# Masking the attention scores: a fill by the vector engine ahead of the row maxima, in place of two products on TensorE

## The chip, the cores and the metric

The kernel runs on one core of a Trainium2 chip. A core has engines that run side by side, each through its own list of instructions in order: TensorE (PE in the profile; PEld is its loading of weights) multiplies matrices, VectorE (DVE) and ScalarE (ACT) work on elements, GpSimd (POOL) does small jobs, and SyncE (SP) starts transfers. They wait for each other by counting semaphores. Products land in PSUM, a memory of eight banks that DVE and ACT read and write too; everything else lies in SBUF.

The metric is the device time of one execution in microseconds (us): before the change 1562.58 us, the median of three runs (1562.52 to 1562.68).

## The reference

Two transformer blocks over 512 tokens of width 1024. The change touches only the attention of the first block. There 16 meta tokens stand in front of the 512, and each of 8 heads has two maps of queries and keys (64 wide) and a value of 128. A token sees the meta tokens and all chunks of 64 tokens up to its own:

```python
cid = jnp.where(pos < N_META, 0, (pos - N_META) // CHUNK + 1)
...
s = jnp.einsum('bqhmd,bkhmd->bhmqk', qb, kf)
mask = cid[None, :] <= qc[:, None]
p = jax.nn.softmax(jnp.where(mask, s, NEG_INF), axis=-1)
a = p[:, :, 0] - lam * p[:, :, 1]
return jnp.einsum('bhqk,bkhe->bqhe', a, vf)
```

Queries are taken 128 at a time, which is two chunks. Against the keys up to the end of their own 128 tokens, the first 64 queries may not see the last 64 keys; the rest of that rectangle is allowed. So per tile of 128 queries and per map the mask is one square: query rows 0 to 63 by the last 64 key columns.

## The kernel before

The program is one fixed list of instructions for each engine, written by hand. Stages follow one another: a convolution's inputs (the GLU), then ten turns that make q, k, v and a gate for each head and do the attention of the head before, then the projections of block one, its feed-forward part, and block two. Weights come in pieces of 512 KB; ACT copies each into a high part (`wh`, line 1405), DVE subtracts to get a low part (`wl`, line 1956), and PE multiplies three times (high by high, high by low, low by high; line 677).

Turn h (lines 927 to 963 on PE) makes the four parts of head h, `part(h, 0)` to `part(h, 3)` (q, k, v, gate), 48 products each, and between them does the attention of head a = h - 1, in four tiles t of 128 queries. A part goes to one PSUM tile (`psP[0]`) that ACT must have emptied (`empty`, line 1483) before the next part begins. The steps of head a:

- `scores(a, t)` on PE (line 837): q by k for both maps, into `psS`. Then, for each map, the product of two constants `mki` and `mkk` (line 858) adds -1e30 to the masked square. At t = 0 the meta tokens' own scores follow (line 861).
- `maxima(a, t)` on DVE (line 2089): the row maxima of both maps in one reduction (line 2093; line 2095 for t = 3; line 2098 for the meta rows).
- `exps(a, t)` on ACT (line 1501): exponentials and their sums, which need the maxima.
- `combine(a, t)` on DVE (line 2101): the difference of the two maps. PE transposes it (`probs`, line 879), ACT copies it, PE multiplies by the values (`outputs`, line 894).
- the norm of head a - 1's output runs through the same turn: `variances` (DVE, 2119), a square root on ACT (`norm_outputs`, 1547), `roots` (DVE, 2126), a scaling on ACT (1553).

What fixes the order around the change: in each turn DVE does maxima 0 and 1, the gate of an earlier head, combine 0 and 1, the low part of a weight piece, four taps of the depthwise convolution (line 2059, 31 taps in each of eight groups, spread over the turns by fixed counts), variances, two taps, maxima 2, roots, combine 2, five taps, maxima 3, three taps, combine 3, a second low part, seven taps. ACT does exps 0 and 1, the high part of a piece, the copy and squares of a head's output, `empty(h, 0)`, the values, exps 2, a copy, the square root (with a load of its function table), the scaling, `empty(h, 1)`, a copy, exps 3, another high part, `empty(h, 2)`, a copy, `empty(h, 3)`. So `part(h, 2)` on PE, which needs `empty(h, 1)`, stands behind maxima 2 by way of ACT. `own` is a helper that makes an engine wait until its own last instruction has finished.

Of the kernel before, what the change touches and what calls it, by code (L numbers as in the profile page):

```python
# [20 lines left out]
T = S + NM  # L21
HT = T // 2
# [11 lines left out]
BIG = 1.0e30  # L34
# [67 lines left out]
def program(nc, A, out):  # L102
    f32, f32r = mybir.dt.float32, mybir.dt.float32r
# [5 lines left out]
    def evacuated(gi):  # L109

        return EV[gi], CREDIT + EV[:gi + 1].count(EV[gi])
# [8 lines left out]
    with ExitStack() as ctx:  # L120
# [25 lines left out]
        scores_ps = ctx.enter_context(nc.psum_tensor("psS", [128, 4, 512], f32))  # L146
# [5 lines left out]
        def at(name, shape, dt=f32, start=None):  # L152
            if start is not None:
                place[0] = start
            n = 4
            for d in shape[1:]:
                n *= d
            t = nc.alloc_sbuf_tensor_at(name, shape, dt, offset=place[0])
            place[0] += -(-n // 32) * 32
            assert place[0] <= nc.sbuf_usable_end, (name, place[0] - nc.sbuf_usable_end)  # L160
            return t
# [27 lines left out]
        PW = [NM + 128 * (t + 1) for t in range(TT)]  # L189
# [32 lines left out]
        pmeta = at("pmeta", [NM, 2, NM])  # L222
        stat = at("stat", [128, 32])
        var = at("var", [128, 2, TT + 1])
        mki = at("mki", [128, 128], f32r)
        mkk = at("mkk", [128, 64], f32r)

# [236 lines left out]
        def span(t, g, c0, n):  # L466

            if isinstance(g, int):
                return t[:, g, c0:c0 + 2 * n].rearrange("p (a b) -> p a b", a=2)
            return t[:, ds(g, 1), c0:c0 + 2 * n].rearrange("p o (a b) -> p (o a) b", a=2)  # L470
# [178 lines left out]
        def _(pe):  # L649
            mm, tr = nc.tensor.matmul, nc.tensor.transpose  # L650
# [134 lines left out]
            for k in range(KT):  # L785
                tr(scores_ps[:, 3, 128 + NM * k:128 + NM * (k + 1)], mn[:, 128 * k:128 * (k + 1)], ident[0:NM, 0:NM])
                ins = tr(scores_ps[:, 3, 256 + NM * k:256 + NM * (k + 1)], mrow[:, 128 * k:128 * (k + 1)], ident[0:NM, 0:NM])
# [10 lines left out]
            for k in range(KT):  # L798
# [3 lines left out]
                for half in range(2):  # L802
                    for p, (W, Y) in enumerate(((wh, xh), (wh, xl), (wl, xh))):
                        for a in range(2):
                            ins = mm(psP[half][:, a, 0:HT], W[:, 0, half, k, :], Y[:, k, a * HT:(a + 1) * HT],  # L805
                                     start=(k == 0 and p == 0), stop=(k == KT - 1 and p == 2))
# [15 lines left out]
            for b in range(2):  # L822
                for v in range(4):
                    o = (4 * b + v) * 2 * FG
                    ins = tr(psP[0][:, 1, o:o + 2 * FG], frow[:, b, v, :], ident[0:2 * FG, 0:2 * FG])
# [11 lines left out]
            def scores(a, t):  # L837
                if a:
                    pe.wait_ge(s_ex, 4 * a + (0, 0, 1, 3)[t])
                elif t >= 2:  # L840
                    pe.wait_ge(s_ex, t - 1 if t == 2 else 3)
                if t == 0:
                    pe.wait_ge(s_ea, evacuated(2 * (N_HEAD + 2 * a) + 1)[1])
                maps = [slice(64 * m, 64 * m + 64) for m in range(2)]
                last = []
                for m, P in enumerate(maps):
                    q = qkv[P, a % 2, 0, NM + 128 * t:NM + 128 * (t + 1)]
                    K = qkv[P, a % 2, 1, :]
                    if t < 3:
                        bank = scores_ps[:, 2 * (t % 2) + m, :]  # L850
                        mm(bank[:, 0:PW[t]], q, K[:, 0:PW[t]], start=True, stop=False)
                        last.append(bank[:, PW[t] - 64:PW[t]])
                    else:
                        mm(scores_ps[:, 2 * m, 0:HT], q, K[:, 0:HT], start=True, stop=True)
                        mm(scores_ps[:, 2 * m + 1, 0:HT], q, K[:, HT:T], start=True, stop=False)
                        last.append(scores_ps[:, 2 * m + 1, HT - 64:HT])
                for m, P in enumerate(maps):
                    ins = mm(last[m], mki[P, :], mkk[P, :], start=False, stop=True)
                if t == 0:
                    for m, P in enumerate(maps):  # L860
                        ins = mm(scores_ps[0:NM, m, PW[0]:PW[0] + NM], qkv[P, a % 2, 0, 0:NM], qkv[P, a % 2, 1, 0:NM], start=True,
                                 stop=True)
                ins.then_inc(s_qk, 1)
# [63 lines left out]
            for h in range(NH + 2):  # L927
                a, b, c = h - 1, h - 2, h - 3
                if b >= 0:
                    probs(b, 3)  # L930
                if 0 <= a < NH:
                    scores(a, 0)
                    scores(a, 1)
# [12 lines left out]
                if 0 <= a < NH:  # L946
                    if h < NH:
                        values(a)
                    scores(a, 2)
                    probs(a, 0)  # L950
# [998 lines left out]
        def _(dve):  # L1949
            V = nc.vector  # L1950
            own = Own(dve, s_v)
# [83 lines left out]
            for z in (vm, pm, vr):  # L2035
                V.memset(z[:], 0.0)
            V.memset(var[:], 1.0)
            V.memset(mki[:].bitcast(f32), 0.0)
            own(V.memset(mkk[:].bitcast(f32), 0.0))
            for m in range(2):  # L2040
                V.memset(mki[64 * m:64 * m + 1, 0:64].bitcast(f32), 1.0)
                V.memset(mkk[64 * m:64 * m + 1, :].bitcast(f32), -BIG)


            tap = [0]
# [43 lines left out]
            def maxima(a, t):  # L2089
                dve.wait_ge(s_qk, 4 * a + t + 1)  # L2090
                if t < 3:
                    b = 2 * (t % 2)
                    ins = V.tensor_reduce(stat[:, 2 * t:2 * t + 2], scores_ps[:, b:b + 2, 0:PW[t]], AX, ALU.max, negate=True)  # L2093
                else:
                    ins = V.tensor_reduce(stat[:, 6:8], scores_ps[:, :, 0:HT].rearrange("p (m a) b -> p m a b", m=2),
                                          mybir.AxisListType.XY, ALU.max, negate=True)
                if t == 0:
                    ins = V.tensor_reduce(stat[0:NM, 16:18], scores_ps[0:NM, 0:2, PW[0]:PW[0] + NM], AX, ALU.max, negate=True)
                ins.then_inc(s_ma, 1)
# [39 lines left out]
            for h in range(NH + 2):  # L2139
                n, a, b, c = N_HEAD + 2 * h, h - 1, h - 2, h - 3  # L2140
                if 0 <= a < NH:
                    maxima(a, 0)
                    maxima(a, 1)
# [15 lines left out]
                if 0 <= a < NH:  # L2159
                    maxima(a, 2)  # L2160
# [34 lines left out]
            for n in range(N_CO, N_CO + 4):  # L2195
                lo(n + 1)
                for half in range(2):
# [3 lines left out]
                    t = nf[:, g % 2, 0:T3]  # L2201
                    if g >= 2:
                        dve.wait_ge(s_ml, g - 1)
                    ins = V.scalar_tensor_tensor(t.rearrange("p (a b) -> p a b", a=2), span(sgc, g, 0, H3), 1.0,
                                                 ALLP[gi % 4][:, :, 0:H3], ALU.add, ALU.mult)
# [418 lines left out]
            for k in range(1, KT):  # L2624
                ins = V.tensor_tensor(sacc[:, 0, 0:S], sacc[:, 0, 0:S] if k > 1 else ysq[:, 0, :], ysq[:, k, :], ALU.add)
# [60 lines left out]
```

## Time and profile before

| | us |
|---|---|
| median of three runs | 1562.58 |
| span of the profiled execution | 1562.9 |
| PE busy | 1532.4 |
| DVE busy | 1126.0 |
| ACT busy | 665.2 |

The profile gives the profiled execution's time as the span from its first to its last instruction, 1562.9 us, 0.3 us above the median of the runs; nothing outside the span is listed. A row of the time order is: start, length, engine, line, operation, output and inputs, shapes, how many are merged, and in brackets the idle time before it with what ended it. A window's row is: from and to, length, busy time and count of PE, PEld, DVE, ACT and POOL, the granted clock of PE (1.00 is full), the transfers' share and GB/s. Lengths of single products are modelled, so PE's cost is better read from one start to the next.

### The profile page before, as it was taken

To read this page: it belongs to the slowest core of one execution; us is meant where nothing else is said; L and a number is where in the kernel's file an instruction comes from. 1 tells how busy PE (TensorE), PEld (TensorE's weight loads), DVE (VectorE), ACT (ScalarE), POOL (GpSimd) and SP (SyncE) were. 2 spreads that over 40 slices of the span, in tenths; PEclk is the share of its full clock that TensorE was granted. 3 is DMA by queue.
4 is the path that set the end of the run, shared out by engine and by line. 5 is a ranking of instruction groups with operands and counts; after the bars stand their busy time and mean duration, and the time that the engine had idled before them with its cause. 6 is when DMAs were issued, how large, how long until landed. Compare 5 with 4: busy or idle time off the path is not lost.

```text
span 1562.9 us, 25443 instructions
## 1 busy us (share of the span) xinstructions
PE 1532.4 (98%) x9972; PEld 1368.4 (88%) x9972; DVE 1126.0 (72%) x1590; ACT 665.2 (43%) x1035; POOL 35.3 (2%) x66
## 2 busy tenths in 40 slices
PE   7999999999999999999999999999999999999998
PEld 7998988898999999999988888878788888888887
DVE  5899888888655577777774548897748988787123
ACT  5223455556662443334333344753646432333112
POOL 0000000100000000000000001000000000000000
PEclk9999999999999999999999999999999999999999
DMA  6323222222223333232223243322122233232321
GB/s 176 82 81 91 72 55 55 55 73 64 68 68 103 87 86 103 81 106 82 77 70 108 77 121 87 81 54 68 55 82 81 81 107 106 82 107 94 108 81 54
DMA packets 235295, 131.63 MB, mean 84 GB/s; under 512 B 20921, under 2 KB 228677, under 8 KB 235221
## 3 DMA queue, kind: packets, MB, share of 16 engines
q1 hardware_dynamic: 234836, 130.40, 29.7%
q8 instruction: 52, 0.85, 0.2%
q0 software_dynamic: 384, 0.20, 0.1%
q14 instruction: 23, 0.18, 0.0%
HBM read 128.48 MB, written 2.10 MB: 84 GB/s over the span
## 4 chain that ended last, share of the span: by engine, by line
PE 77%; DVE 15%; ACT 6%; issue 1%; DMA 0%; DVEq 0%; ACTq 0%
PE psP L677 25%; PE psS L677 22%; PE psP L742 8%; DVE conv L2059 7%; PE psS L1353 4%; PE psP L1353 4%; PE psP L699 4%; PE psP L1044 3%; DVE wl L1956 2%; PE psP L1221 1%; ACT prob L1512 1%; PE psS L1221 1%; ACT wh L1405 1%; PE psP L805 1%; DVE stat L2093 1%
## 5 line engine op out<-in xcount | busy, mean ns | idle before, releaser
L1956 DVE TENSOR_TENSOR wl<-raw,wh 128x2048 fp32r<-128x2048 f32 x124 | 284.1, 2291 | 178.3 <-ACT wh L1405 176.5
L677 PE MATMUL psP<-xh,wh 128*128 128x258 f32 (+2 forms) x1296 | 320.3, 312 | 13.8 <-ACT qkv L1499 8.9
L1405 ACT ACTIVATE wh<-raw 128x2048 fp32r<-128x2048 f32 x124 | 237.2, 1913 | 209.5 <-PE psS L1353 74.3
L677 PE MATMUL psP<-xh,wl 128*128 128x258 f32 (+2 forms) x1296 | 315.9, 308 | 0.0
L677 PE MATMUL psP<-xl,wh 128*128 128x258 f32 (+2 forms) x1296 | 315.3, 308 | 0.0
L677 PEld LDWEIGHTS psP<-xh,wh 128*128 128x128 f32 x1296 | 211.8, 191 | 30.3 <-issue 8.0
L677 PEld LDWEIGHTS psP<-xl,wh 128*128 128x128 f32 x1296 | 211.3, 190 | 12.0 <-issue 0.2
L677 PEld LDWEIGHTS psP<-xh,wl 128*128 128x128 f32 x1296 | 211.2, 190 | 11.9
L677 PE MATMUL psS<-xh,wh 128*128 128x258 f32 (+2 forms) x768 | 186.7, 307 | 0.4 <-DVE hT L1985 0.4
L677 PE MATMUL psS<-xh,wl 128*128 128x258 f32 (+2 forms) x768 | 185.9, 307 | 0.0
L677 PE MATMUL psS<-xl,wh 128*128 128x258 f32 (+2 forms) x768 | 185.6, 306 | 0.0
L2059 DVE SCALAR_TENSOR_TENSOR conv<-u,cdw,conv 128x516 f32<-128x516 f32 x232 | 175.0, 754 | 6.4
L677 PEld LDWEIGHTS psS<-xh,wh 128*128 128x128 f32 x768 | 124.6, 189 | 8.0 <-DVE hT L1985 0.7
L677 PEld LDWEIGHTS psS<-xl,wh 128*128 128x128 f32 x768 | 124.3, 189 | 7.1
L677 PEld LDWEIGHTS psS<-xh,wl 128*128 128x128 f32 x768 | 124.1, 189 | 7.0
L1642 ACT ACTIVATE acth<-prod 128x512 f32 x44 | 27.7, 630 | 196.4 <-DVE prod L2269 196.4
L2263 DVE SCALAR_TENSOR_TENSOR acc<-upr,fdw,acc 128x512 f32<-128x512 f32 x88 | 66.2, 752 | 12.2 <-DVE acc L2262 6.4
L2264 DVE SCALAR_TENSOR_TENSOR acc<-upr,fdw,acc 128x512 f32<-128x512 f32 x88 | 66.2, 752 | 12.1 <-DVE acc L2263 6.4
L742 PE MATMUL psP<-actl,wh 128*128 128x512 f32 x176 | 69.6, 396 | 0.0
L742 PE MATMUL psP<-acth,wl 128*128 128x512 f32 x176 | 69.6, 395 | 0.0
L742 PE MATMUL psP<-acth,wh 128*128 128x512 f32 x176 | 69.6, 395 | 0.0
L2262 DVE TENSOR_SCALAR acc<-upr,fdw 128x512 f32<-128x512 f32 x88 | 48.1, 547 | 17.1 <-DVE upr L2259 16.8
(463 smaller groups left out, 2440.1 us busy)
## 6 DMA issues: line engine op xcount, KB each, us to landing
raw<-in_w_in_dram SPq DMA_DIRECT2D x76, 512.0 KB, 5.0
raw<-in_w_up_dram SPq DMA_DIRECT2D x44, 512.0 KB, 4.9
raw<-in_ffn_up_dram SPq DMA_DIRECT2D x44, 512.0 KB, 5.0
raw<-in_ffn_down_dram SPq DMA_DIRECT2D x22, 512.0 KB, 4.1
raw<-in_w_out_dram SPq DMA_DIRECT2D x16, 512.0 KB, 4.7
raw<-in_w_down_dram SPq DMA_DIRECT2D x16, 384.0 KB, 3.6
raw<-in_w_down_dram SPq DMA_DIRECT2D x16, 320.0 KB, 4.0
raw<-in_w_conv_out_dram SPq DMA_DIRECT2D x8, 512.0 KB, 4.6
```

The source lines that it names most:

```text
L677: ins = mm(ps[0:rows, a, 0:nn], W[:, s, half, k, 0:rows], Y[:, k, c0 + a * nn:c0 + (a + 1) * nn], start=(k == 0 and p == 0), stop=(k == KT ...
L699: ins = mm(ps[0:r, a, 0:nn], W[:, s, half, k, 0:r], Y[:, k, c0 + a * nn:c0 + (a + 1) * nn], start=(k == 0 and p == 0), stop=(k == KT - 1 a ...
L742: ins = mm(ps[:, 0, :], W[:, k, :], Y[:, kk, :], start=(kk == 0 and p == 0), stop=(kk == FG - 1 and p == 2))
L1044: ins = mm(psP[0][:, half, 256 * a:256 * (a + 1)], Y[:, k, o:o + 128], W[:, n % 2, :, k, :], start=(k == 0 and p == 0), stop=(k == KT - 1 ...
L1221: ins = mm(ZP[t][c], Y[:, k, tok], w, start=(k == 0 and p == 0), stop=(k == KT - 1 and p == 2))
L1353: ins = mm(ALLP[t][:, half, :], Y[:, kk, tok], W[:, j, :], start=(kk == 0 and p == 0), stop=(kk == FG - 1 and p == 2))
L1405: fn(wh[:, n % 2], raw[:, n % 2], ACT.Copy).then_inc(s_hi, 1)
L1956: V.tensor_tensor(wl[:, n % 2], raw[:, n % 2], wh[:, n % 2].bitcast(f32), ALU.subtract).then_inc(s_lo, 1)
L2059: own(V.scalar_tensor_tensor(y, src, w, y, ALU.mult, ALU.add))
L2262: own(V.tensor_scalar(acc[:, x, :], upr[:, j, x, 4:4 + S], w[2], w[3], ALU.mult, ALU.add))
L2263: own(V.scalar_tensor_tensor(acc[:, x, :], upr[:, j, x, 3:3 + S], w[1], acc[:, x, :], ALU.mult, ALU.add))
L2264: V.scalar_tensor_tensor(acc[:, x, :], upr[:, j, x, 2:2 + S], w[0], acc[:, x, :], ALU.mult, ALU.add).then_inc(s_cva, 1)
```

## The change

The two products with `mki` and `mkk` per tile are gone, with the constants and the four fills that set them at the start. In `maxima`, after the wait for the scores, DVE fills the masked square of both maps with -1e30 in one instruction (64 partitions by 2 by 64 elements, in PSUM), waits until that is done, and then reduces as before.

```diff
@@ scores(a, t), PE
                     if t < 3:
                         bank = scores_ps[:, 2 * (t % 2) + m, :]
-                        mm(bank[:, 0:PW[t]], q, K[:, 0:PW[t]], start=True, stop=False)
-                        last.append(bank[:, PW[t] - 64:PW[t]])
+                        ins = mm(bank[:, 0:PW[t]], q, K[:, 0:PW[t]], start=True, stop=True)
                     else:
                         mm(scores_ps[:, 2 * m, 0:HT], q, K[:, 0:HT], start=True, stop=True)
-                        mm(scores_ps[:, 2 * m + 1, 0:HT], q, K[:, HT:T], start=True, stop=False)
-                        last.append(scores_ps[:, 2 * m + 1, HT - 64:HT])
-                for m, P in enumerate(maps):
-                    ins = mm(last[m], mki[P, :], mkk[P, :], start=False, stop=True)
+                        ins = mm(scores_ps[:, 2 * m + 1, 0:HT], q, K[:, HT:T], start=True, stop=True)
@@ setting of constants, DVE
-            V.memset(mki[:].bitcast(f32), 0.0)
-            own(V.memset(mkk[:].bitcast(f32), 0.0))
-            for m in range(2):
-                V.memset(mki[64 * m:64 * m + 1, 0:64].bitcast(f32), 1.0)
-                V.memset(mkk[64 * m:64 * m + 1, :].bitcast(f32), -BIG)
@@ maxima(a, t), DVE
                 dve.wait_ge(s_qk, 4 * a + t + 1)
                 if t < 3:
                     b = 2 * (t % 2)
+                    own(V.memset(scores_ps[0:64, b:b + 2, PW[t] - 64:PW[t]], -BIG))
                     ins = V.tensor_reduce(stat[:, 2 * t:2 * t + 2], scores_ps[:, b:b + 2, 0:PW[t]], AX, ALU.max, negate=True)
                 else:
+                    own(V.memset(scores_ps[0:64, :, HT - 64:HT].rearrange("p (m a) b -> p m a b", m=2)[:, :, 1, :], -BIG))
                     ins = V.tensor_reduce(stat[:, 6:8], scores_ps[:, :, 0:HT].rearrange("p (m a) b -> p m a b", m=2),
                                           mybir.AxisListType.XY, ALU.max, negate=True)
```

How DVE's list stands at maxima 0 and 1 of head 1, before (`psS` holds the scores, `stat` the maxima; in brackets the semaphores that an instruction waits for, `dve_own_steps` being DVE's wait for itself):

```order
L2059 SCALAR_TENSOR_TENSOR conv<-u,cdw,conv 128x516 [waits dve_own_steps] x6
L2093 TENSOR_REDUCE stat<-psS 128x2 [waits scores_ready,dve_own_steps]
L2098 TENSOR_REDUCE stat<-psS 16x2
L2093 TENSOR_REDUCE stat<-psS 128x2 [waits scores_ready]
L2108 RECIPROCAL stat<-stat 16x1 [waits exps_ready]
```

The same place of the changed list (its lines 2081 and 2082 are the fill and the reduction, 2088 the meta rows, 2098 the reciprocal):

```order
L2047 SCALAR_TENSOR_TENSOR conv<-u,cdw,conv 128x516 [waits dve_own_steps] x6
L2081 MEMSET psS 64x2x64 [waits scores_ready,dve_own_steps]
L2082 TENSOR_REDUCE stat<-psS 128x2 [waits dve_own_steps]
L2088 TENSOR_REDUCE stat<-psS 16x2
L2081 MEMSET psS 64x2x64 [waits scores_ready]
L2082 TENSOR_REDUCE stat<-psS 128x2 [waits dve_own_steps]
L2098 RECIPROCAL stat<-stat 16x1 [waits exps_ready]
```

The wait for the scores now stands on the fill, and each reduction waits for the fill in front of it.

Maxima 2 and 3 of the same head on DVE, before, with the steps between (`var` is the norm's root, `prob` the combined tile):

```order
L2093 TENSOR_REDUCE stat<-psS 128x2 [waits scores_ready,dve_own_steps]
L2126 RECIPROCAL var<-var 128x5 [waits head_roots]
L2108 RECIPROCAL stat<-stat 128x1 [waits exps_ready]
L2109 SCALAR_TENSOR_TENSOR stat<-stat,nlam 128x1 [waits dve_own_steps]
L2110 SCALAR_TENSOR_TENSOR prob<-prob_70,stat,prob 128x400 [waits dve_own_steps]
L2059 SCALAR_TENSOR_TENSOR conv<-u,cdw,conv 128x516
L2059 SCALAR_TENSOR_TENSOR conv<-u,cdw,conv 128x516 [waits dve_own_steps] x4
L2095 TENSOR_REDUCE stat<-psS 128x2 [waits scores_ready,dve_own_steps]
```

And in the changed list:

```order
L2081 MEMSET psS 64x2x64 [waits scores_ready,dve_own_steps]
L2082 TENSOR_REDUCE stat<-psS 128x2 [waits dve_own_steps]
L2116 RECIPROCAL var<-var 128x5 [waits head_roots]
L2098 RECIPROCAL stat<-stat 128x1 [waits exps_ready]
L2099 SCALAR_TENSOR_TENSOR stat<-stat,nlam 128x1 [waits dve_own_steps]
L2100 SCALAR_TENSOR_TENSOR prob<-prob_70,stat,prob 128x400 [waits dve_own_steps]
L2047 SCALAR_TENSOR_TENSOR conv<-u,cdw,conv 128x516
L2047 SCALAR_TENSOR_TENSOR conv<-u,cdw,conv 128x516 [waits dve_own_steps] x4
L2084 MEMSET psS 64x2x64 [waits scores_ready,dve_own_steps]
L2085 TENSOR_REDUCE stat<-psS 128x2 [waits dve_own_steps]
```

One fill is added at each; nothing else on DVE changes place.

PE's list at scores 0 and 1 of head 1, before (`mkk,mki` are the mask's products, `psP<-vm` the first of the head's outputs):

```order
L851 MATMUL psS<-qkv 128x144 [waits emptied_by_act,exps_ready]
L851 MATMUL psS<-qkv 128x144
L858 MATMUL psS<-mkk,mki 128x64 x2
L861 MATMUL psS<-qkv 16x16 x2
L851 MATMUL psS<-qkv 128x272 [waits exps_ready]
L851 MATMUL psS<-qkv 128x272
L858 MATMUL psS<-mkk,mki 128x64 x2
L890 MATMUL psP<-vm,aTp 16x128 [waits attention_copied]
```

After the change:

```order
L848 MATMUL psS<-qkv 128x144 [waits emptied_by_act,exps_ready]
L848 MATMUL psS<-qkv 128x144
L854 MATMUL psS<-qkv 16x16 x2
L848 MATMUL psS<-qkv 128x272 [waits exps_ready]
L848 MATMUL psS<-qkv 128x272
L883 MATMUL psP<-vm,aTp 16x128 [waits attention_copied]
```

Two products fewer per tile, eight per head, 64 in all; the order of the rest is as it was.

## Rows read from the trace of the kernel before

**Rows 1.** The page, busy time of each engine: share of the span, instructions.

```profile
PE 1532.4 (98%) x9972; PEld 1368.4 (88%) x9972; DVE 1126.0 (72%) x1590; ACT 665.2 (43%) x1035; POOL 35.3 (2%) x66
```

**Rows 2.** Windows from maxima 0 of one head to the next: heads 1, 3, 6.

```profile
178.19:214.44 36.25, 33.98 (x267) 31.60 (x265) 29.45 (x50) 19.66 (x48) 1.80 (x5) 0.95 0.22 59
249.28:283.53 34.25, 32.87 (x266) 30.46 (x266) 29.50 (x51) 19.71 (x48) 3.29 (x5) 1.00 0.23 62
353.21:387.29 34.08, 33.11 (x272) 30.55 (x270) 29.39 (x51) 19.69 (x48) 3.30 (x5) 1.00 0.23 63
```

**Rows 3.** DVE in time order: maxima 0 and 2 of head 2, then head 4.

```profile
214.44 0.46 DVE L2093 TENSOR_REDUCE stat<-psS 128x2 f32<-128x288 f32 x1 [1.43 <-PE psS L861]
...
226.98 0.99 DVE L2093 TENSOR_REDUCE stat<-psS 128x2 f32<-128x800 f32 x1
...
283.53 0.46 DVE L2093 TENSOR_REDUCE stat<-psS 128x2 f32<-128x288 f32 x1
...
288.19 2.29 DVE L1956 TENSOR_TENSOR wl<-raw,wh 128x2048 fp32r<-128x2048 f32 x1 [0.47 <-ACT wh L1405]
...
296.67 0.99 DVE L2093 TENSOR_REDUCE stat<-psS 128x2 f32<-128x800 f32 x1
...
300.68 0.19 DVE L2126 RECIPROCAL var<-var 128x5 f32<-128x5 f32 x1 [3.02 <-ACT var L1547]
...
305.70 1.26 DVE L2095 TENSOR_REDUCE stat<-psS 128x2 f32<-128x1056 f32 x1
...
318.37 0.46 DVE L2093 TENSOR_REDUCE stat<-psS 128x2 f32<-128x288 f32 x1
```

**Rows 4.** ACT in time order, head 4: exps 0, exps 2, the emptying before `part(5, 2)`.

```profile
284.11 0.38 ACT L1512 ACTIVATE prob<-psS,stat 128x144 f32<-128x144 f32 x1 [0.62 <-DVE stat L2098]
...
297.70 0.60 ACT L1512 ACTIVATE prob<-psS,stat 128x400 f32<-128x400 f32 x1 [1.40 <-DVE stat L2093]
...
303.44 0.58 ACT L1499 ACTIVATE qkv<-psP 128x528 f32<-128x528 f32 x1
```

**Rows 5.** PE in time order: scores 0 of head 4, `part(5, 2)`, scores 0 of head 5.

```profile
282.62 0.52 PE L851 MATMUL psS<-qkv 64*128 64x144 f32 x4
...
304.17 0.48 PE L677 MATMUL psP<-xh,wh 128*128 128x264 f32 x2 [1.05 <-ACT qkv L1499]
...
317.44 0.52 PE L851 MATMUL psS<-qkv 64*128 64x144 f32 x4
```

**Rows 6.** PE in time order, head 1: the mask's products and what follows them.

```profile
177.40 0.29 PE L858 MATMUL psS<-mkk,mki 64*128 64x64 f32 x2
177.62 0.22 PE L861 MATMUL psS<-qkv 64*16 64x16 f32 x4
...
188.88 0.50 PE L858 MATMUL psS<-mkk,mki 64*128 64x64 f32 x2
189.31 0.33 PE L879 MATMUL psP<-ident,prob 128*128 128x128 f32 x1
```

**Rows 7.** DVE in time order: fills; the one at 36.53 is waited for.

```profile
36.40 0.17 DVE L2038 MEMSET mki<- 128x128 f32 x1
36.53 0.11 DVE L2039 MEMSET mkk<- 128x64 f32 x1
36.71 0.11 DVE L2041 MEMSET mki<- 1x64 f32 x1
```

**Rows 8.** PE in time order: `part(2, 2)` in head 1 and scores 0 of head 2.

```profile
198.83 0.48 PE L677 MATMUL psP<-xh,wh 128*128 128x264 f32 x2 [1.90 <-ACT qkv L1499]
...
213.63 0.52 PE L851 MATMUL psS<-qkv 64*128 64x144 f32 x4
```

**Rows 9.** Windows: just after `part(2, 2)` began, and the stages after the heads.

```profile
199.00:202.60 3.60, 3.60 (x19) 3.60 (x19) 3.50 (x5) 0.96 (x4) 0.00 (x0) 0.54 0.02 5
...
410.00:560.00 150.00, 149.74 (x1233) 148.36 (x1233) 85.91 (x99) 66.96 (x86) 0.20 (x1) 1.00 0.31 85
```

**Rows 10.** PE in time order: the first part of turn 8, head 7's.

```profile
394.37 0.50 PE L677 MATMUL psP<-xh,wh 128*128 128x258 f32 x2 [0.43 <-ACT nf L1574]
```

More of the change, by code:

```diff
@@ L224, in program @@
         var = at("var", [128, 2, TT + 1])
-        mki = at("mki", [128, 128], f32r)
-        mkk = at("mkk", [128, 64], f32r)
         ch = at("ch", [128, KT, S], f32r, start=base)
@@ L844, in scores @@
                 maps = [slice(64 * m, 64 * m + 64) for m in range(2)]
-                last = []
                 for m, P in enumerate(maps):
```

## The prediction
> **What bounds the kernel now.** The page first: PE is busy 1532 of 1562.9 us [rows 1], so one would look for PE's time and expect that taking products away helps. The stages after the heads bear that out: from 410 to 560 us PE is busy 149.74 of 150 [rows 9]. But the change lies in the turns of the heads, and there the windows, the second view, read otherwise: PE is idle 2.27, 1.38 and 0.97 us in the turns of heads 1, 3 and 6, and in head 1's the granted clock is 0.95 on the mean [rows 2]. So in that stage something else sets the length of a turn.
>
> The time order of DVE, ACT and PE over one turn, head 4's, shows what. Three ways run through it.
>
> The way through DVE: from maxima 0 at 283.53 to the next at 318.37 are 34.84 us [rows 3], and DVE stands still for only two things, 0.47 us for a weight copy of ACT and 3.02 us for the square root. Both hang on DVE itself: ACT starts exps 0 and exps 2 on the maxima, having waited 0.62 and 1.40 us for them [rows 4], and the weight copy and the root come behind these in ACT's list. So DVE with ACT's replies closes a loop without PE. Heads 2 and 5 also take 34.84 us, by the starts in rows 3 and 2; head 3 takes 34.25, head 6 34.08 [rows 2].
>
> The way through PE: maxima 2 at 296.67, exps 2, root, scaling, `empty` at 303.44, PE's `part(5, 2)` at 304.17 after 1.05 us of idle, scores 0 of the next head at 317.44 [rows 3 to 5]. That is 7.50 and 13.27 us. Where DVE waits for PE, the reduction starts 0.81 us after scores 0 (213.63 to 214.44), and maxima 2 follows 12.54 us later (13.14 in head 4, which has more of the convolution between) [rows 3, 8]. Sum 34.12: 0.7 under the 34.84 of the first way. The two are nearly level.
>
> The way through PE at half clock: in head 1 `part(2, 2)` began after 1.90 us of idle and needed 14.80 us to the next scores 0 [rows 8] in place of 13.27, since PE ran at a mean granted clock of 0.54 from 199.0 to 202.6 [rows 9], that is mostly at the lower level, 1.2 GHz. That turn took 36.25 us and DVE waited 1.43 for PE [rows 2, 3].
>
> **The change part by part.** *PE's products go.* From the first of a pair to the next instruction are 0.22 us at t = 0 and 0.43 at t = 2 [rows 6]; t = 1 and t = 3 I take between them. That is 1.3 us a head, 10.4 in all eight. All of it lies ahead of `part(h, 2)`, where PE already waits for ACT, except the 0.22 of t = 0, which lies on the way through PE. So of each 1.3 us at most 0.22 is saved and the rest makes PE's idle longer, in heads 0 to 6.
>
> *DVE's fills come.* None into PSUM is in the trace. A fill of 64 elements that is waited for takes 0.18 us to the next start; one of 128 elements is 0.05 to 0.06 longer by its own length (0.17 to 0.11) [rows 7]. That gives 0.23. From below: 0.13, the step from a 128-element fill to the next without a wait [rows 7]; a gain is excluded, since the reduction behind it is unchanged. From above: reductions that read PSUM take 0.99 us for 800 elements and 0.46 for 288 [rows 3], 1.04 ns an element and 0.16 fixed, so 0.29 for 128, and 0.03 for the wait: 0.32. I take 0.23, the nearest row.
>
> The Trainium skill, "PSUM — Partial Sum Buffer" (Specifications), gives 1.04 ns per element for a VectorE fill of 2-byte elements into PSUM on trn2, and says that the fill's own row doesn't show it. No run here shows that yet; the fills of rows 7 grow by 0.8 to 0.9 ns an element. By the page the estimate would be 0.03 us more per fill, some 0.5 us in the sum.
>
> *Which fills show.* The fill of t = 0 delays exps 0 and with it ACT's weight copy: counted. That of t = 1 hides: it lies beside exps 0 on ACT, and DVE's 0.47 us of waiting for the copy takes it up [rows 3]. That of t = 2 stands before exps 2, the root and the 3.02 us: counted. That of t = 3 delays the combination, the second low part and the next maxima 0, and DVE waits for nobody there: counted. Without the 0.47, t = 1 would cost 0.23 a head as well, 1.6 in seven. So the way through DVE grows by 3 x 0.23 = 0.69 us a turn.
>
> *The sum without any more half clock.* Heads 2 to 5, and head 0, whose turn goes through DVE alone too: five times 0.69, 3.45. Head 1, set by PE: fills 0 and 2 less the 0.22, 0.24. From head 6 on the turns have no convolution left; there PE waits 0.43 us only for ACT's copy of the means [rows 10]. Between a gain of head 7's 1.3 us of products and a loss of another 0.69 I take a loss of 0.4, since that copy stands in ACT's list behind exps 0 and 1 of head 7. Sum 4.1 us. After that PE is back to back [rows 9], so nothing is given back.
>
> *The clock.* PE's idle before `part(h, 2)` grows. In head 4: scores 0 to the start of the idle were 304.17 - 1.05 - 282.62 = 20.50, now 19.2; with 13.27 behind it and a turn of 35.53, 3.1 us are idle; at half clock, in a turn of 36.49, 2.5; in the other heads down to about 1.9. Before, the one idle of this place that reached 1.90 was followed by half clock [rows 8, 9], and head 4's 1.05 was not: its products kept the full pace [rows 5], and heads 3 and 6 show 1.00 for the whole turn [rows 2]. If a head falls, its way through PE is 7.50 + 14.80 + 0.81 - 0.22 + 0.23 + 12.54 + 0.23 = 35.89 us (36.49 where 13.14 stands for 12.54), against 35.53, 34.94, 35.53 and 35.53 through DVE in heads 2 to 5. That is 0.36, 0.95, 0.96 and 0.36 more, and about 1.0 in head 6, where 0.5 of the 1.53 is hidden in ACT's lateness (an estimate): 3.65 if all five fall. The idles lie between the one that cost the clock and a half more, so I count two thirds, 2.4 us.
>
> The Trainium skill, "TensorE: Matmul & The Clock Gate" (HAM oscillation — how this bites in real kernels), tells of loops whose matmuls wait in every turn and start every turn cold. Here one turn of the heads before did so; that all will is the second rival.
>
> *The fills at the start* that set the constants go too, about 0.6 us of DVE by the steps of rows 7; PE has its own transposes and products there, so I take nothing. On the path, it would be a gain of 0.6.
>
> Forecast: 1562.9 + 4.1 + 2.4 = 1569.4 on the profiled execution; the median lies 0.3 below the span, so 1569.1 us, 6.5 us (0.4%) slower.
>
> **The rivals.** *No new half clock.* The lengthened idle leaves the clock at 1.00 and only the fills count: 4.1 us, 1566.7; with fills at 0.13 (18 of them on the path, 0.1 each) 1564.8, at 0.32 1568.3. For it: idles of up to 1.05 us left no trace. Against it: 1.90 did.
>
> *Half clock in every head, and dearer fills.* 4.1 + 3.65 = 7.75 us, 1570.3; with fills at 0.32 1.6 more, 1571.9.
>
> *PE sets the turns after all* (faster). If DVE's 3.02 us were slack, because the root were released by something earlier than exps 2, the fills would vanish in it and PE would save its 1.3 us a head: 1562.6 - 10.4 = 1552.2. It decides from the point where PE's idle before `part(h, 2)` is used up. Against it: ACT works through exps 2 and the table load in just that time, after waiting for DVE [rows 4].
>
> *No change.* Fills cost their least, head 7 gains its 1.3 us and the clock stays: under 3 us.
>
> **How the numbers follow.** About 0.2%, 3.1 us, is what a measurement of this kernel can tell from no change. Forecast, with some heads at half clock (5 to 7.5 us): 0.54. No new half clock (2 to 5 us): 0.25, of which 0.08 lies under 3.1. Every head and dear fills (over 7.5 us): 0.11. PE sets the turns: 0.06. No change: 0.04. So faster 0.06, same 0.12, slower 0.82. The range reaches down into the rival with cheap fills and up to the dearest case: 1564.9 to 1571.8.
>
> **What would show it.** Right: turns from maxima 0 to maxima 0 of 35.4 to 36.5 us where there were 34.1 to 34.8; a fill-to-reduction step of 0.23 us; ACT's waits for the maxima longer by a fill at t = 0, 2 and 3, DVE's 0.47 us wait shorter; PE's idle before `part(h, 2)` at 2 us and more, with granted clocks below 1.00 in several turns; from 425 us on the same lengths, started later. Wrong: turns as long as before or shorter, with PE's idle unchanged; a fill step far from 0.23; or turns longer while PE's idle stays near 1 us, which would mean that I have the wrong engine.

## The result, and the profile after

The changed kernel takes 1569.74 us, the median of five runs (1568.24 to 1570.80); the kernel before takes 1562.68. The ratio is 1.0038, with an interval of 1.0026 to 1.0051: 0.4% slower, against a forecast of 1569.1 in a range of 1564.9 to 1571.8. The profiled execution of the changed kernel spans 1568.0 us and is the run of 1569.74, so 1.74 us lie around its span. Executions of one and the same kernel fall into two groups about 1.8 us apart, which go with whether a head falls to half clock (PE's granted clock drops from 1.00 to about 0.5 for a few us of its turn): of 50 executions of the kernel before, 23 took 1562.3 to 1562.8 us (granted clock 0.997 to 0.998) and 27 took 1563.9 to 1564.9 (0.996), and its profiled execution, with a span of 1562.9, is of the second group while its median is of the first.

First the page's line of busy time, after (engine, busy us, share of the span, instructions):

```profile
PE 1531.3 (98%) x9908; PEld 1362.6 (87%) x9908; DVE 1130.7 (72%) x1616; ACT 663.5 (42%) x1035; POOL 36.0 (2%) x66
```

Against [rows 1] 64 products have gone and PE is 1.1 us less busy, 0.02 us a product; DVE is 4.7 us busier.

Next the windows of the changed kernel, which answer to [rows 2] and [rows 9]: the turns of heads 1, 2, 3, 4 and 6 from reduction to reduction, a stretch behind `part` in head 3, and the stages after the heads. The columns are window, length, busy time and instructions of PE, PEld, DVE, ACT and POOL, granted clock, DMA share, GB/s.

```profile
179.05:214.66 35.61, 32.59 (x259) 29.59 (x258) 30.19 (x54) 19.57 (x48) 3.43 (x5) 1.00 0.22 60
214.66:250.27 35.61, 33.94 (x269) 30.58 (x267) 30.77 (x56) 19.57 (x48) 3.54 (x5) 1.00 0.22 60
250.27:286.39 36.12, 34.00 (x259) 31.18 (x258) 30.17 (x55) 19.68 (x48) 2.05 (x5) 0.95 0.21 59
286.39:322.00 35.61, 33.55 (x267) 30.15 (x264) 30.77 (x55) 19.68 (x48) 3.44 (x5) 1.00 0.22 60
...
357.67:392.56 34.89, 33.24 (x264) 30.16 (x262) 30.12 (x55) 19.56 (x48) 3.44 (x5) 1.00 0.23 61
270.60:274.00 3.40, 3.40 (x16) 3.40 (x17) 3.24 (x5) 0.49 (x3) 0.00 (x0) 0.51 0.02 5
...
410.00:566.00 156.00, 155.74 (x1281) 153.78 (x1280) 90.30 (x108) 72.69 (x98) 0.79 (x2) 1.00 0.30 82
```

Each turn that half clock lengthens in neither kernel is 0.76 to 0.83 us longer than before: head 2 35.61 for 34.84, head 6 34.89 for 34.08 [rows 2]. Head 1 is shorter, 35.61 for 36.25, because its clock is now 1.00 where it was 0.95; head 3 is 1.87 longer, because it has the 0.95 now. Head 0's turn has a stretch at half clock in both (0.92 and 0.93), but it is 31.56 us long at 0.95 as well (the kernel with neither, told of below), so the clock doesn't set it. The seven turns add up as follows (us; the kernel with one fill, told of below, gives head 1 at full clock without the change, 34.83):

| head | before | after | of it fills | of it clock |
|---|---|---|---|---|
| 0 | 31.56 | 32.32 | +0.76 | |
| 1 | 36.25 | 35.61 | +0.78 | -1.42 |
| 2 | 34.84 | 35.61 | +0.77 | |
| 3 | 34.25 | 36.12 | +0.79 | +1.08 |
| 4 | 34.84 | 35.61 | +0.77 | |
| 5 | 34.84 | 35.67 | +0.83 | |
| 6 | 34.08 | 34.89 | +0.81 | |
| sum | 240.66 | 245.83 | +5.51 | -0.34 |

Of head 3's 1.87 I count 0.79 as fills, the mean of the other six. Ahead of the first turn 0.10 us is added (first maxima 0 at 146.73 for 146.63). That is the first fill, 0.25, less a start that is 0.15 earlier: DVE's third split of weights begins at 29.93 for 30.08, and from there to maxima 0 are 116.80 us for 116.55. Behind the last turn 0.17 goes (1175.44 us from maxima 0 of head 7 to the end, for 1175.61, with spans given to 0.1). Together 5.10, the difference of the spans.

DVE in time order after the change, head 4 and the start of head 5, answering to [rows 3] (start, duration, engine, line, operation, tiles, idle before and its releaser):

```profile
286.19 0.17 DVE L2081 MEMSET psS<- 64x128 f32 x1 [1.20 <-PE psS L854]
286.39 0.46 DVE L2082 TENSOR_REDUCE stat<-psS 128x2 f32<-128x288 f32 x1
...
286.96 0.17 DVE L2081 MEMSET psS<- 64x128 f32 x1
287.16 0.72 DVE L2082 TENSOR_REDUCE stat<-psS 128x2 f32<-128x544 f32 x1
...
291.04 2.29 DVE L1949 TENSOR_TENSOR wl<-raw,wh 128x2048 fp32r<-128x2048 f32 x1 [0.33 <-ACT wh L1398]
...
299.59 0.17 DVE L2081 MEMSET psS<- 64x128 f32 x1
299.79 0.99 DVE L2082 TENSOR_REDUCE stat<-psS 128x2 f32<-128x800 f32 x1
...
303.79 0.19 DVE L2116 RECIPROCAL var<-var 128x5 f32<-128x5 f32 x1 [3.01 <-ACT var L1540]
...
308.88 0.17 DVE L2084 MEMSET psS<- 64x128 f32 x1
309.07 1.26 DVE L2085 TENSOR_REDUCE stat<-psS 128x2 f32<-128x1056 f32 x1
...
322.00 0.46 DVE L2082 TENSOR_REDUCE stat<-psS 128x2 f32<-128x288 f32 x1
```

A fill begins 0.19 to 0.20 us ahead of its reduction. It also begins later than the reduction did: root to fill 3 is 5.09 us (303.79 to 308.88), root to maxima 3 was 5.02 [rows 3]. So a fill that counts costs 0.27, and three make 0.81. The reductions behind the fills are as long as before. The wait for the square root is unchanged (3.01 for 3.02), that for the weight copy is 0.33 for 0.47. For PE, DVE waits in this stretch only once, the 1.20 us at 286.19, at the end of head 3's turn with the lower clock.

ACT after, exps 0, exps 2 and the emptying of head 4, answering to [rows 4]:

```profile
286.97 0.38 ACT L1505 ACTIVATE prob<-psS,stat 128x144 f32<-128x144 f32 x1 [0.74 <-DVE stat L2088]
...
300.81 0.60 ACT L1505 ACTIVATE prob<-psS,stat 128x400 f32<-128x400 f32 x1 [1.87 <-DVE stat L2082]
...
306.55 0.58 ACT L1492 ACTIVATE qkv<-psP 128x528 f32<-128x528 f32 x1
```

ACT waits longer for the maxima, 1.87 for 1.40 ahead of exps 2 and 0.74 for 0.62 ahead of exps 0, as the prediction had it for a turn that DVE sets.

PE after, in time order: `part` of heads 1, 3 and 4, then scores 0, 1 and 2 of head 5, answering to [rows 5], [rows 6] and [rows 8]:

```profile
199.94 0.48 PE L675 MATMUL psP<-xh,wh 128*128 128x264 f32 x2 [2.53 <-ACT qkv L1492]
...
270.55 0.69 PE L675 MATMUL psP<-xh,wh 128*128 128x264 f32 x2 [1.75 <-ACT qkv L1492]
...
307.28 0.48 PE L675 MATMUL psP<-xh,wh 128*128 128x264 f32 x2 [1.55 <-ACT qkv L1492]
...
320.69 0.52 PE L848 MATMUL psS<-qkv 64*128 64x144 f32 x4
321.14 0.22 PE L854 MATMUL psS<-qkv 64*16 64x16 f32 x4
...
321.94 0.66 PE L893 MATMUL psP<-ident,otok 128*128 128x128 f32 x4
...
332.64 0.94 PE L848 MATMUL psS<-qkv 64*128 64x400 f32 x4
333.51 0.33 PE L872 MATMUL psP<-ident,prob 128*128 128x128 f32 x1
```

Two things here are not as forecast. From the scores' start to what follows are 0.45 us at t = 0 and 0.87 at t = 2; in head 4 before they were 0.47 (282.62 to 283.09) and 0.90 (294.60 to 295.50), with the mask's products in between. So taking a pair away saved 0.02 to 0.03 us there. And PE's idle before `part` grew from 1.05 to 1.55 in head 4, not to 3.1. Of the three idles shown, that of 2.53 us was followed by full clock and that of 1.75 by half clock.

### The profile page after: what moved, and what is told of

Its sections match the earlier page's. It is cut to its first block, busy times and chain, and to the rows that moved or that the text cites. A ratio compares the mean times of both kernels' runs of the same rounds, so it can differ in the third digit from the quotient of the medians.

```text
span 1568.0 us, 25341 instructions
## 1 busy us (share of the span) xinstructions
PE 1531.3 (98%) x9908; PEld 1362.6 (87%) x9908; DVE 1130.7 (72%) x1616; ACT 663.5 (42%) x1035; POOL 36.0 (2%) x66
## 4 chain that ended last, share of the span: by engine, by line
PE 76%; DVE 17%; ACT 6%; issue 1%; DMA 0%; DVEq 0%; ACTq 0%
PE psP L675 24%; PE psS L675 22%; PE psP L740 8%; DVE conv L2047 8%; PE psS L1346 4%; PE psP L1346 4%; PE psP L697 4%; PE psP L1037 3%; DVE wl L1949 3%; PE psP L1214 1%; ACT prob L1505 1%; PE psS L1214 1%; ACT wh L1398 1%; PE psP L803 1%; DVE stat L2082 1%
```

## The experiments

All kernels below ran against the kernel before. A head that falls to half clock lengthens its turn, so the turns at full clock, read from each kernel's profile, are compared first.

**Neither products nor fills.** From the changed kernel both fills are taken out; the mask is left out of the scores.

```diff
-                    own(V.memset(scores_ps[0:64, b:b + 2, PW[t] - 64:PW[t]], -BIG))
...
-                    own(V.memset(scores_ps[0:64, :, HT - 64:HT].rearrange(...)[:, :, 1, :], -BIG))
```

> Neither the products nor the fills; the mask is left out of the computation. Theory (DVE with ACT's replies sets the turn, the products cost PE next to nothing, 0.03 us a pair): turns of 34.1 to 34.8 us as before wherever the clock is full, PE's idle before part(h, 2) larger by 0.1 us, time within 1 us of before but for turns at half clock. Rival from the prediction (a pair costs PE 0.3 us): PE's idle there larger by 1.0 to 1.3 us, so 2.0 to 2.4 in heads 3 and 4, and head 7's tail 1 us shorter. Rival (PE sets the turn): 8 to 10 us faster.

Measured: 1562.49 us, ratio 0.9999 (0.9990 to 1.0009). The turns are 31.56, 34.83, 34.84, 34.23, 34.84, 34.84 and 34.04: those of before, where it has full clock, to 0.04 us. PE in time order, `part` of head 4:

```profile
302.15 0.48 PE L675 MATMUL psP<-xh,wh 128*128 128x264 f32 x2 [1.13 <-ACT qkv L1492]
```

The idle is 1.13 us for 1.05 with eight more products in the head. So the products and the fills for their constants were worth nothing that shows in time, and the whole loss comes from the fills.

**Both.** The kernel before, with the fills put in ahead of its reductions.

```diff
+                    own(V.memset(scores_ps[0:64, b:b + 2, PW[t] - 64:PW[t]], -BIG))
                     ins = V.tensor_reduce(stat[:, 2 * t:2 * t + 2], ...)
...
+                    own(V.memset(scores_ps[0:64, :, HT - 64:HT].rearrange(...)[:, :, 1, :], -BIG))
                     ins = V.tensor_reduce(stat[:, 6:8], ...)
```

> Products and fills both. Theory: every full-clock turn as long as after the change, 34.9 to 35.7 us (0.8 more than before), time within 1 us of after, since only the fills count. Rival (removing the products gave PE something that was part of the result): 1 to 3 us away from after. Rival (the larger idle after the change cost half clock): fewer half-clock turns than after, up to 2.4 us under it.

Measured: 1570.12 us, ratio 1.0043 (1.0028 to 1.0057). Heads 2 to 6 take 35.63, 35.00, 35.62, 35.66 and 34.88, the changed kernel's turns (head 3 at full clock). With the products kept the fills cost the same. The medians are 0.4 us apart, the spans of the profiled executions 1.1 (1569.1 and 1568.0): here heads 0 and 1 fall to half clock (33.63 and 36.78, 1.31 and 1.17 longer than there) and head 3 doesn't (1.12 shorter). So keeping the products didn't spare the half clock, which one rival expected.

**The same fill, elsewhere.** The kernel before, with fills of equal shape into a tile in SBUF that isn't in use at that time, waited for in the same way.

```diff
+                    own(V.memset(rstd[0:64, 0:128].rearrange("p (m c) -> p m c", m=2), -BIG))
                     ins = V.tensor_reduce(...)
...
```

> Products kept; the fill of 64 by 128 elements goes to an unused SBUF tile, with the same wait, ahead of each reduction. Theory (a fill with its wait costs 0.27 us in DVE's order wherever it writes): turns and time as with products and fills in PSUM, 0.8 us a turn. Rival (writing PSUM is the dear part): step under 0.22 us, turns 0.5 us or less over before.

Measured: 1569.65 us, ratio 1.0039 (1.0025 to 1.0054). DVE in time order, the fill and the reduction of maxima 2:

```profile
299.79 0.17 DVE L2093 MEMSET rstd<- 64x128 f32 x1
299.99 0.99 DVE L2094 TENSOR_REDUCE stat<-psS 128x2 f32<-128x800 f32 x1
```

0.20 us from fill to reduction, as into PSUM, and the turns agree to 0.1 us. What costs is one more short instruction that is waited for in DVE's list; where it writes makes no difference here. No run has a fill that isn't waited for, so how much of the cost is the wait isn't shown.

**One fill, in the place with a wait.** The kernel before with only the products of t = 1 replaced by their fill.

```diff
+                    if t == 1:
+                        own(V.memset(scores_ps[0:64, b:b + 2, PW[t] - 64:PW[t]], -BIG))
...
-                for m, P in enumerate(maps):
+                for m, P in enumerate(maps if t != 1 else []):
```

> The kernel before with only the products of t = 1 replaced by a fill. Theory (that fill hides in DVE's 0.47 us wait for the weight copy): that wait falls to about 0.1 us, turns within 0.05 us of before at full clock, time within 1 us of the like runs of before. Rival (every fill counts): 0.27 us a turn, 2 us.

Measured: 1563.26 us, ratio 1.000 (0.999 to 1.001). The turns are 31.54, 34.83, 34.83, 34.23, 34.83, 34.83 and 34.07. DVE in time order, head 5:

```profile
316.86 0.17 DVE L2094 MEMSET psS<- 64x128 f32 x1
317.06 0.72 DVE L2095 TENSOR_REDUCE stat<-psS 128x2 f32<-128x544 f32 x1
...
320.94 2.29 DVE L1956 TENSOR_TENSOR wl<-raw,wh 128x2048 fp32r<-128x2048 f32 x1 [0.32 <-ACT wh L1405]
```

The fill is there, and the wait for the weight copy went from 0.47 to 0.32, not to the 0.1 expected. It doesn't lengthen the turn: one fill in four hides, as the prediction counted. The rest of it is taken up before: in head 4 the gate's step begins 1.41 us behind maxima 0, where it was 1.25. In heads 0 and 1 that wait stays at 0.47 to 0.48, and the one for ACT's meta rows falls instead, from 0.76 to 0.43.

**Each fill twice.** The changed kernel, with every fill issued two times, each waited for.

```diff
                     own(V.memset(scores_ps[0:64, b:b + 2, PW[t] - 64:PW[t]], -BIG))
+                    own(V.memset(scores_ps[0:64, b:b + 2, PW[t] - 64:PW[t]], -BIG))
...
```

> The changed kernel with each fill done twice, each waited for. Theory (three of the four fills of a turn lie on DVE's loop, the one of t = 1 mostly hides in the 0.33 us that DVE waits for the weight copy): a second fill takes 0.20 us to the next start, so 0.6 us a full-clock turn more than after the change, 4 to 5 us in all. Rival (all four lie on it): 0.8 a turn, 5.6. Rival (fills run beside other work): under 2.

Measured: 1576.68 us, ratio 1.0082 (1.0064 to 1.0100), 6.9 over the changed kernel. The windows of heads 1, 2 and 4, in the profiled execution:

```profile
181.48:218.77 37.29, 34.11 (x260) 31.11 (x258) 30.85 (x58) 19.68 (x48) 2.29 (x5) 0.95 0.21 57
218.77:255.18 36.41, 34.19 (x271) 30.76 (x269) 31.44 (x60) 19.57 (x48) 3.55 (x5) 1.00 0.22 59
290.99:328.23 37.24, 34.50 (x263) 31.31 (x260) 31.45 (x59) 19.68 (x48) 2.36 (x5) 0.95 0.21 58
```

DVE in time order, maxima 2:

```profile
304.23 0.17 DVE L2081 MEMSET psS<- 64x128 f32 x1
304.49 0.17 DVE L2082 MEMSET psS<- 64x128 f32 x1
304.69 0.99 DVE L2083 TENSOR_REDUCE stat<-psS 128x2 f32<-128x800 f32 x1
```

From fill to fill are 0.26 us, from fill to reduction 0.20: this is the 0.27 by which a fill counts. Head 2 is again 0.80 longer (36.41 for 35.61), heads 5 and 6 0.81 and 0.79, so the second set costs what the first did. The 0.6 expected was too low, and 0.8 is the number of the rival in which all four fills lie on the loop; the trace tells the two apart. In head 2 maxima 2 begins 13.08 us behind maxima 0, for 12.79 after the change: 0.29 more for the second fills of t = 1 and t = 2 together, while the wait of 0.33 for the weight copy is used up. The two stretches behind it grow by 0.26 and 0.25. So three fills still count, at 0.26 each, and that of t = 1 hides all but 0.03.

Heads 0, 1 and 4 take 0.8 to 1.1 more than the 0.80; the clock of these turns is 0.89, 0.95 and 0.95. The spans of the profiled executions are 8.1 apart (1576.1 and 1568.0): 5.6 for seven second sets, 1.8 for three heads at half clock (2.84) in place of one (1.08), and the rest ahead of the first turn and behind the last.

**The products twice.** The kernel before, with each pair of the mask's products issued two times.

```diff
-                for m, P in enumerate(maps):
-                    ins = mm(last[m], mki[P, :], mkk[P, :], start=False, stop=True)
+                for r in range(2):
+                    for m, P in enumerate(maps):
+                        ins = mm(last[m], mki[P, :], mkk[P, :], start=False, stop=r == 1)
```

> The kernel before with the pair of mask products issued twice in each tile. Theory (a pair takes its place in a gap that PE has anyhow, and PE waits for ACT in each turn): first pair free, the second at most 0.1 to 0.2 us a tile, PE's idle before part(h, 2) smaller by 0.3 to 0.7 us a turn, full-clock turns within 0.1 us, time within 1.5 us of like runs of before. Rival (products set the time): 0.33 us a tile, 1.3 a turn, 10 us slower.

Measured: 1563.01 us, ratio 1.000 (0.999 to 1.001). PE in time order at scores 2 of head 4, first the kernel before, then this one:

```profile
294.60 0.94 PE L851 MATMUL psS<-qkv 64*128 64x400 f32 x4
295.06 0.50 PE L858 MATMUL psS<-mkk,mki 64*128 64x64 f32 x2
295.50 0.33 PE L879 MATMUL psP<-ident,prob 128*128 128x128 f32 x1
```

```profile
292.79 0.94 PE L851 MATMUL psS<-qkv 64*128 64x400 f32 x4
293.25 0.61 PE L859 MATMUL psS<-mkk,mki 64*128 64x64 f32 x4
293.80 0.33 PE L880 MATMUL psP<-ident,prob 128*128 128x128 f32 x1
```

From the scores' start to the transpose: 0.90 with one pair, 1.01 with two, 0.87 with none. The second pair costs 0.11 us, the first 0.03. The turns keep their 34.84, and only head 6's is longer, 34.20 for 34.08; PE's idle before `part` of head 4 falls from 1.05 to 0.60, four times 0.11. So the products lie in PE's idle, and even twice as many are covered but for that 0.1.

**One step of the convolution less, after and before.** In the turns of heads 0 to 6, one of DVE's convolution steps a turn (0.75 us) is left out, of the changed kernel and of the kernel before; the convolution lacks these terms.

```diff
+                    if j >= 100 and (j - 100) % 21 == 0:
+                        continue
                     if k < CK - 1:
                         own(V.scalar_tensor_tensor(y, src, w, y, ALU.mult, ALU.add))
```

> The changed kernel with one convolution step on DVE left out in each of the turns 1 to 7, 0.79 us each; the convolution is incomplete. Theory (DVE's own list sets the turn): turns shorter by 0.79 us, back to 34.1 to 34.9, time 4.5 to 5.5 us under after, about that of before. Rival (PE or half clock sets the turns by now): less than 2 us under after.

> The kernel before with one convolution step on DVE left out in each of the turns 1 to 7; the convolution is incomplete. Theory (DVE sets the turn by 34.84 us and PE's way comes 0.7 behind): full-clock turns shorter by 0.5 to 0.79 us, to 34.1 or so, PE's idle before part(h, 2) near its 0.35 us least, time 3 to 5.5 us under before. Rival (the two ways are tied elsewhere): under 2 us.

Measured: after, 1565.28 us, ratio 1.0011 (1.0002 to 1.0021), 4.5 under the changed kernel. Heads 0, 2 and 5 give back 0.79 to 0.81, a whole step (2 and 5: 34.82 and 34.86), heads 1 and 4 only 0.37 to 0.38: their 35.23 and 35.24 are longer than expected. The seven turns sum to 240.84, where the changed kernel's, less head 3's half clock, sum to 244.75. Before, 1560.36 us, ratio 0.9981 (0.9972 to 0.9991); the turns are 30.77, 34.75, 34.14, 34.14, 34.73, 34.14 and 34.08, with full clock in all but head 0's (0.95). They sum to 236.75, for 239.16 in the kernel with one fill, which has no turn lengthened by half clock either: 2.4 us less, under the 3 to 5.5 expected and not far from the rival's 2. Heads 0, 2 and 5 give back 0.77, 0.69 and 0.69, the others 0.1 or nothing. DVE in time order at the end of head 3's turn, first in the kernel after and then in the kernel before, and the window of that turn in the latter:

```profile
282.31 0.17 DVE L2083 MEMSET psS<- 64x128 f32 x1 [0.50 <-PE psS L854]
```

```profile
279.93 0.46 DVE L2095 TENSOR_REDUCE stat<-psS 128x2 f32<-128x288 f32 x1 [0.74 <-PE psS L861]
```

```profile
245.79:279.93 34.14, 33.42 (x272) 30.82 (x272) 28.82 (x49) 19.81 (x49) 2.51 (x5) 1.00 0.23 62
```

DVE now waits 0.74 us for PE: the way through PE is what is late next. The prediction had worked it out of rows as 34.12 us, and with head 4's 13.14 us for 12.54 it is 34.72; measured are 34.14, and 34.73 to 34.75 in heads 4 and 1. With the fills it is longer, 35.23 and 35.24 in these heads, and DVE waits 0.49 to 0.50 for PE at the ends of heads 1, 3, 4 and 6. That the shorter list shortens the turn until the way through PE is met shows which engine sets it.

## Why the prediction was right, and where its sizes were off

**Which engine sets the turn: right.** Both kernels of the last pair shorten their turns when only DVE's list is shortened, and doubling PE's products moves nothing. The rival in which PE sets the turns falls with these. But the margin of 0.7 us holds for heads 2 and 5 alone. The prediction set head 4's 34.84 through DVE against a way through PE with head 2's 12.54; with head 4's own 13.14 the margin is 0.12, and in heads 1, 3, 4 and 6 a shorter list gives back 0.1 us or nothing before PE's way is met. That the fills still cost 0.8 there comes from where they stand: those of t = 0 and t = 2 lengthen the way through PE as well, by about 0.5 (35.23 for 34.74), and that of t = 3 the way through DVE alone.

**Three fills of four: right, and each mis-sized by 0.04.** The one at t = 1 alone costs nothing, and a full set costs 0.76 to 0.83 a turn where 0.69 was forecast. The step of 0.23 was taken from fill to next start [rows 7]; measured are 0.20, and in maxima 3 0.07 that come on top because the fill begins later behind the convolution's step than the reduction did. The fill's own row and its step are the same into SBUF, so the bound from reductions reading PSUM had no part in it. The Trainium skill, "PSUM — Partial Sum Buffer" (Specifications), gives 1.04 ns an element for 2-byte fills into PSUM, from which the prediction had estimated 0.03 more per fill; the two kernels with 4-byte fills show no such difference.

**PE's products: the step that failed.** The prediction took the pitch from the first product to the next instruction, 0.22 to 0.43 us [rows 6], as what a pair costs. Most of that pitch stays when the pair is gone: 0.03 us a pair was saved, some 0.1 a head in place of 1.3. The pair starts before the scores ahead of it are through (their modelled end in head 4 is 295.54, the pair starts at 295.06), and the pitch holds their end. So of PE's idle before `part`, forecast at 1.9 to 3.1 us in heads 2 to 6, only 1.15 to 1.75 came about (head 1: 2.53); 0.50 to 0.83 of it is new, about as much as the turn's own growth. For the same reason the prediction's sign of a wrong engine, longer turns with PE's idle near 1 us, is met in heads 2, 5 and 6 (1.15 to 1.19) although the engine was right.

**The clock: mis-sized.** Forecast were 2.4 us more, for two thirds of five heads falling behind idles that would exceed 1.90 in most of them. The idles stayed shorter, and one head fell in the profile, head 3; its price was near the forecast, 1.08 for 0.95. With head 1 no longer falling, the clock gave 0.34 us back on the profiled executions. So this came nearer to the rival without new half clock, with its fills at the dear end. Length of idle isn't what decides: head 1 of before fell behind 1.90 us [rows 8, 9], but the kernel with neither had 1.96 there and the one with one fill 1.92, both at full clock; the changed kernel kept full clock behind 2.53 and fell behind 1.75. In the ten profiles together, idles of 1.65 to 2.81 us before `part` were followed by half clock, and others of up to 2.59 by full clock. PE in head 1, the kernel with neither and then the one with one fill:

```profile
198.25 0.48 PE L675 MATMUL psP<-xh,wh 128*128 128x264 f32 x2 [1.96 <-ACT qkv L1492]
```

```profile
198.20 0.48 PE L677 MATMUL psP<-xh,wh 128*128 128x264 f32 x2 [1.92 <-ACT qkv L1499]
```

By the times the fills still seem to bring half clock more often, as the prediction argued. Of 19 executions with all fills in the full list (after, both, fill in SBUF, fills twice) 18 took about 1 us or more over what the fills account for, and the four that were profiled have a fallen head; of 79 of the kernels without them (before, neither, one fill, products twice) 38 did. Why, and in which head, the times alone don't say.

The Trainium skill, "TensorE: Matmul & The Clock Gate" (HAM oscillation — how this bites in real kernels), speaks of loops that start cold in every turn; of the changed kernel's seven turns one was slowed by it, and the rival with half clock in every head is wrong.

**Head 1, head 6 and the tail.** Head 1 was costed at 0.24 on the ground that PE set it; at full clock DVE does, and its fills cost 0.78. Head 6 and what lies behind were put at 0.4; measured 0.81 - 0.17 = 0.64. For the fill ahead of the very first maxima 0 the prediction has no term; it costs 0.25. The fills in all: 5.51 + 0.25 = 5.76, or 5.59 with the 0.17 behind the last turn, for 4.1.

**The sum, and what lies around the span.** Span by span the change is 5.10 (5.59 - 0.34, less the 0.15 by which the profiled start is earlier), where 6.5 was forecast: dear fills and a missing clock term partly cancel. The median of before was taken to lie 0.3 under the profiled span; in fact every run whose span is on record lies 1.7 to 1.8 us above it, and the profiled execution of before, with head 1 at half clock, isn't like the median one. From median to median the change is 7.06: the fills' 5.6 to 5.8, head 3's 1.08 of half clock in the changed kernel's median execution, and about 0.4 for a later start that goes with it (29.93 for 29.5, below). At equal clock the difference has the fills' size: the one execution of the changed kernel at 0.998 took 1568.24 us, 5.7 more than the 1562.58 that is the median of before at 0.997 to 0.998. The forecast hit 1569.1 for 1569.74 because a span forecast 1.4 too high met an offset taken 2.04 too low. The sign and the engine are shown; the closeness of the number is luck.

## What to carry to other kernels

The time from a short instruction's start to the next is not its price: remove it or double it in thought, and ask what the neighbours would wait for anyway. Before work is moved from the busiest engine to a less busy one, find which engine's list sets the turn of that stage; here PE at 98% had idle to spare and DVE at 72% had none in three places of four. A short waited-for step cost its row and its hand-overs on both sides here, 0.27 us for a row of 0.17, times the places where its engine waits for nobody.

## What the runs showed of the hardware

A second pair of 64-row products of 64 columns behind the scores costs 0.11 us, the first 0.03, at t = 0, 1 and 2 alike to 0.02 (heads 4 and 5: starts 0.47, 0.69 and 0.90 apart with one pair; 0.58, 0.80 and 1.01 with two; 0.45, 0.66 and 0.87 with none).

Whether a head falls to half clock goes with when TensorE first reaches its full pace. In the five profiled executions without a fallen head (neither, one fill, products twice, and both with a step less) twelve transposes at 14 us take 1.53 us and the first two products behind them 0.48; in the five with one (before, after, both, fill in SBUF, fills twice) these two products take 0.69 to 0.78, and the transposes are slower too. (All ten run at half clock around the first maxima 0, which isn't counted here.) PE in time order, the kernel with one fill and then the kernel before:

```profile
13.97 1.53 PE L778 MATMUL psS<-ident,xn 128*128 128x128 f32 x12 [1.02 <-DVE xn L1981]
17.18 0.48 PE L805 MATMUL psP<-xh,wh 128*128 128x264 f32 x2 [1.69 <-DVE xl L1994]
```

```profile
14.14 2.82 PE L778 MATMUL psS<-ident,xn 128*128 128x128 f32 x12 [0.69 <-DVE xn L1981]
17.35 0.78 PE L805 MATMUL psP<-xh,wh 128*128 128x264 f32 x2 [0.39 <-DVE xl L1994]
18.37 0.41 PE L805 MATMUL psP<-xh,wl 128*128 128x264 f32 x2
```

The profile's column of the granted clock shows 1.00 there, so this is read from the pace alone: the transposes take 1.8 times as long, the first products 1.6 times, and from 18.37 on the pace is the same. The delay stays: DVE's third split of weights begins at 29.50 to 29.59 us in the five without a fallen head and at 29.68 to 30.17 in the five with one, and the first maxima 0 is at 146.63 in before and at 146.03 in the kernel with one fill. By that, the position of an idle in time would matter beside its length. Whether the later rise leads to the fall or only goes with it, no run here settles; if the fills change how often a head falls, as the times suggest, it isn't all. The Trainium skill, "TensorE: Matmul & The Clock Gate" (What's actually happening), says that the stretches over which the chip looks at activity run on freely and do not begin with the kernel, which would fit; nothing here shows them.
